# A two-layer hybrid decoder step on one core: the order of the work in both mixes is set anew

## What is computed

```python
def trunk_layer(x, ...):
    h = x @ p['w_in']                                   # 1024 -> 2560, 20 tiles of 128 rows
    u_a, q_b, k_b, v_b, q_c, k_c, v_c, g_c = split(h)   # 2,2,2,2,2,2,4,4 tiles
    ya = rms_norm(s5_branch(u_a, ...))                  # complex diagonal scan, gelu, h*sigmoid(h@w_glu)
    yb = rms_norm(sb_attend(q_b, kb, vb, sb_bias))      # stick-breaking attention, samples read paged K/V
    yc, ret_s = retention_branch(q_c, k_c, v_c, g_c)    # rotary, decay, state, group norm, silu(g)*o
    x = layer_norm(ALPHA * x + concat(ya, yb, yc) @ p['w_out'])
    f = conv_ffn(x, prev, w_up, conv_w, conv_b, w_down) # 1024 -> 5632 -> 2816 -> 1024
    return layer_norm(ALPHA * x + f)
```

## Time and profile before

| | |
|---|---|
| runs, median (lowest to highest) | 739.29 us (739.11 to 741.52), 3 runs |
| the profiled execution | 739.12 us, its span 737.3 us, mean granted clock 0.977 |
| TensorE busy | 678.6 us |
| VectorE busy | 557.2 us |
| ScalarE busy | 407.9 us |
| GpSimd busy | 173.6 us |
| first mix, input norm included | 0 to 142.1 us |
| second mix, from its first raw unit | 377.0 to 498.2 us |

### The profile page before, as it was taken

One profiled execution on the slowest core, in us unless ns is written; L12 is line 12 of the kernel. 1 busy time (PEld: TensorE's weight loads), 2 busy tenths in 40 slices (PEclk: granted clock), 3 DMA queues, 4 the chain that ended last, 5 costly groups with the idle time before them and its releaser, 6 DMA issues. The chain is left out here.

```text
span 737.3 us, 13093 instructions
## 1 busy us (share of the span) xinstructions
PE 678.6 (92%) x4950; PEld 623.7 (85%) x4950; DVE 557.2 (76%) x1083; ACT 407.9 (55%) x649; POOL 173.6 (24%) x130
## 2 busy tenths in 40 slices
PE   5999988597999999998999979969899999999994
PEld 4877776496999999997997768759699999999993
DVE  6688975968988888599945997256899888873543
ACT  4766514747666666652367643374576666664343
POOL 0000000344222222644220000024432221245441
PEclk9999999799999999999999999998999999999998
DMA  9666530342756554533347462241375555546511
GB/s 352 192 222 228 169 106 30 115 148 92 235 200 241 181 190 174 184 144 140 146 160 255 164 213 90 88 171 57 116 245 201 176 193 176 183 168 209 170 58 59
DMA packets 43728, 122.41 MB, mean 166 GB/s; under 512 B 5186, under 2 KB 16354, under 8 KB 43154
## 3 DMA queue, kind: packets, MB, share of 16 engines
q1 hardware_dynamic: 39746, 115.55, 45.1%
q0 software_dynamic: 704, 3.06, 1.4%
q10 hardware_dynamic: 3216, 2.97, 1.2%
HBM read 116.05 MB, written 5.51 MB: 165 GB/s over the span
## 5 line engine op out<-in xcount | busy, mean ns | idle before, releaser
L388 PE MATMUL ps<-x_hi,w_hi 128*128 128x264 f32 x688 | 196.1, 285 | 1.1 <-DVE x_lo L1650 1.1
L389 PE MATMUL ps<-x_lo,w_hi 128*128 128x264 f32 x688 | 194.9, 283 | 0.0
L390 PE MATMUL ps<-x_hi,w_lo 128*128 128x264 f32 x688 | 194.8, 283 | 0.0
L835 ACT CAST w_hi<-ring 128x1024 fp32r<-128x1024 f32 x146 | 151.2, 1041 | 78.4 <-PE ps L390 77.3
L1267 DVE TENSOR_TENSOR w_lo<-ring,w_hi 128x1024 fp32r<-128x1024 f32 x114 | 141.5, 1243 | 39.8 <-ACT w_hi L835 36.8
L381 PE MATMUL ps<-x,ring 128*128 128x264 f32 x576 | 135.6, 391 | 4.5 <-ACT x L923 4.5
L381 PEld LDWEIGHTS ps<-x,ring 128*128 128x128 f32 x576 | 106.2, 190 | 30.4 <-issue 9.1
L388 PEld LDWEIGHTS ps<-x_hi,w_hi 128*128 128x128 f32 x688 | 129.5, 188 | 1.9 <-DVE x_lo L1650 1.5
L389 PEld LDWEIGHTS ps<-x_lo,w_hi 128*128 128x128 f32 x688 | 129.6, 188 | 0.1
L390 PEld LDWEIGHTS ps<-x_hi,w_lo 128*128 128x128 f32 x688 | 129.0, 187 | 0.0
L1719 POOL TENSOR_TENSOR w_lo<-ring,w_hi 128x1024 fp32r<-128x1024 f32 x32 | 78.2, 2450 | 136.9 <-ACT w_hi L835 136.9
(11 more groups left out here) (305 smaller groups left out, 1052.4 us busy)
## 6 DMA issues: line engine op xcount, KB each, us to landing
ring<-in_units SPq DMA_DIRECT2D x188, 512.0 KB, 3.5
kv<-in_kpool SPq DMA_DIRECT2D x32, 128.0 KB, 2.4
kv<-in_vpool SPq DMA_DIRECT2D x32, 128.0 KB, 2.6
SR<-in_sret SPq DMA_DIRECT2D x2, 1024.0 KB, 6.0
out_rsample<-SR POOLq DMA_DIRECT2D x2, 1024.0 KB, 8.0
z<-in_xT SPq DMA_DIRECT2D x2, 528.0 KB, 5.3
out_kv<-hb ACTq DMA_DIRECT2D x2, 528.0 KB, 4.1
out_y<-x SPq DMA_DIRECT2D x2, 528.0 KB, 2.6
```

The costliest lines, as they stand in the source:

```text
L388: mm(out, wh, hi, start=start, stop=False)
L389: mm(out, wh, lo, start=False, stop=False)
L390: return mm(out, wl, hi, start=False, stop=stop)
L835: E.did(nc.scalar.copy(w_hi[:, split_slot(i)], ring[:, ring_slot(n)]), "w_hi")
```

## The change

It moves steps, and makes one in another way. Nothing in what is computed changes, except for how the value rows get to their place.

1. Layer 0, norm: `s5_angle` and `s5_angle2` behind the eight differences; `s5_den` and the third part of the phases in front of `ln_tail_raw`; the fourth part right behind it. ScalarE takes the sines of the constants behind tile 5, and makes the tables of the first half right behind the norm.
2. S5's input projections follow units 5, 6, 9, 10 in layer 0 (before 7, 8, 12, 13) and 2, 3, 6, 7 in layer 1 (before 3, 4, 8, 9), so in layer 1 the first stands within the raw units. `raw_add` of unit 2 comes later.
3. The tables of the second half lie in a place of their own (over RI and KD) and their low part over VT. For layer 1 the turns are made in the down projection of layer 0: ScalarE behind splits 12 to 15, VectorE behind the last residual.
4. All other steps follow other units. The sums rms and gvar now follow unit 18, so unit 19 stands behind them.
5. Silu is taken for three gate tiles ahead of the evacuation of unit 19 and for the fourth behind it (semaphore gsil counts 2); the first four branches are split ahead of the inverse root of the group norm. VectorE's `gn_out` and `branch_lo` alternate. `split_lo` of the fourth w_out unit moves behind them.
6. VS, vs_scratch and the transfers go. `v_samples` multiplies, for each sample and head, a column of v repeated 32 times with the identity; ScalarE copies the two banks to VBC.

```diff
-OUT_BANK = [3, 4, 6, 7]
+OUT_BANK = [4, 5, 6, 7]
-TAB_AT = [(7, 9), (None, 7)]
-TURNS_AT = [(3, 4), (4, 5)]
+TURNS_AT = [[5, 6, 6, 7], [12, 13, 14, 15]]
-AT = [{"ss": 5, "sc": 6, "b00": 7, "b01": 8, "vbt": 9, "b10": 12, "b11": 13, "c0": 13, "vt": 16, "tails": 16,
-       "c1": 18, "glu": 19, "inner": 19, "kt": 19, "values": 19, "rsq": 19, "rt": 19, "out": 19, "sv": 19,
-       "yt": 19, "gmean": 19, "gvar": 19, "rms": 19},
-      {"b00": 3, "b01": 4, "ss": 5, "sc": 6, "b10": 8, "b11": 9, "c0": 9, "vbt": 10, "tails": 12, "c1": 14,
-       "glu": 15, "inner": 16, "kt": 16, "vt": 16, "values": 16, "rsq": 16, "rt": 17, "out": 17, "sv": 17,
-       "yt": 18, "gmean": 18, "gvar": 19, "rms": 19}]
+AT = [{"b00": 5, "b01": 6, "ss": 6, "sc": 7, "tab": 8, "vbt": 8, "b10": 9, "b11": 10, "c0": 10, "logs": 10, "srg": 12,
+       "tails": 14, "c1": 15, "glu": 16, "inner": 17, "kt": 17, "values": 17, "sv": 17, "rsq": 17, "vt": 16,
+       "rt": 18, "yt": 18, "out": 18, "vb": 18, "gmean": 18, "rms": 18, "gvar": 18},
+      {"b00": 2, "b01": 3, "ss": 4, "tab": 4, "sc": 5, "b10": 6, "b11": 7, "c0": 7, "logs": 7, "vbt": 8, "srg": 12,
+       "tails": 10, "c1": 11, "glu": 13, "inner": 13, "kt": 13, "values": 14, "sv": 14, "rsq": 14, "vt": 15,
+       "rt": 15, "yt": 15, "out": 16, "vb": 17, "gmean": 17, "rms": 17, "gvar": 18}]
...
+            def v_samples(L):
+
+                for half in range(2):
+                    bank = claim(2 + half, "vbev", L, half + 1)
+                    for b in range(4):
+                        for h in range(HEADS):
+                            v = hb[:, VC + h, SEQ + 4 * half + b:SEQ + 4 * half + b + 1].to_broadcast([P, 32])
+                            ins = mm(bank[32 * h:32 * h + 32, b * DV:(b + 1) * DV], v, C["ident"], start=True, stop=True,
+                                     tile_position=(0, 32 * h))
+                    E.did(ins, "vb")
...
+                if AT[L]["b00"] < RAW:
+                    s5_evac(L, 0, 0)
+                    neg_c(L)
                 correction(2)
-
-            def s5_turns_up(L, part):
-
-                if part == 0:
+                if L == 0:
+                    s5_tables(L, 0)
+
+            def s5_turns_up(L, jj):
+
+                if jj == 0:
                     act.wait_ge(S("turned"), L + 1)
-                    if L > 0:
-                        need(act, "bb", L, 1)
-                    E.settle()
+                    need(act, "bb", L, 1)
...
             def v_spread(L):
-                act.wait_ge(S("st_vs"), 16 * (L + 1))
-                v4 = vs_dram[L].rearrange("b (h e) -> h b e", h=HEADS)
-                for h in range(HEADS):
-                    act.dma_start(VBC[32 * h:32 * h + 32], v4[h:h + 1].to_broadcast([32, NS, DV])
-                                  ).then_inc(S("ld_vbc"), 16)
+                for half in range(2):
+                    need(act, "vb", L, half + 1)
+                    E.did(nc.scalar.copy(VBC[:, 4 * half:4 * half + 4], ps[:, 2 + half].rearrange("p (b e) -> p b e", b=4)),
+                          "vbev")
...
+                    if i == at_["gvar"]:
+                        for k in range(4):
+                            branch_hi(L, k)
                         need(act, "gvar", L, HEADS)
                         E.did(f(rg[:], ps[:, 4:8, 0:T], ACT.Ln, bias=eps_t[LN_EPS]), "gv1")
                         E.settle()
                         E.did(f(rg[:], rg[:], ACT.Exp, scale=-0.5), "gr")
-                E.settle()
-                E.did(f(hb[:, GC:GC + HEADS], hb[:, GC:GC + HEADS], ACT.Silu), "gsil")
-                for k in range(KT):
+                        E.did(f(hb[:, GC:GC + 3], hb[:, GC:GC + 3], ACT.Silu), "gsil")
+                E.settle()
+                E.did(f(hb[:, GC + 3], hb[:, GC + 3], ACT.Silu), "gsil")
+                for k in range(4, KT):
                     branch_hi(L, k)
+                split_hi(L, N_IN + 3)
...
                         if d in S5_ACT:
                             s5_params(L + 1, S5_ACT.index(d))
+                        for jj in range(HJ):
+                            if d == TURNS_AT[1][jj]:
+                                s5_turns_up(L + 1, jj)
...
-                split_lo(L, N_IN + 2)
-                split_lo(L, N_IN + 3)
                 s5_cat(L)
                 sb_cat(L)
-                gn_out(L)
-                for k in range(4, KT):
-                    branch_lo(L, k)
+                split_lo(L, N_IN + 2)
+                gn_scale(L)
+                gn_out(L, 0)
+                gn_out(L, 1)
+                branch_lo(L, 4)
+                gn_out(L, 2)
+                branch_lo(L, 5)
+                gn_out(L, 3)
+                branch_lo(L, 6)
+                branch_lo(L, 7)
+                split_lo(L, N_IN + 3)
...
+                if L + 1 < DEPTH:
+                    s5_turns_down(L + 1)
             ln_tail(2 * DEPTH)
```

More of the change, by code:

```diff
@@ L196, in hybrid_step @@
         ps = ctx.enter_context(nc.psum_tensor("ps", [P, 8, 512], F32))
-        vs_dram = [nc.dram_tensor(f"vs_scratch{l}", [NS, HEADS * DV], F32, kind="Internal").ap()
-                   for l in range(DEPTH)]
         def pv(L, name, i=0, n=1):
@@ L713, in _ @@
                         vb_transposes(L)
-                    if L == 0 and i == at_["vt"]:
-                        transposes(L)
                     if i == at_["tails"]:
@@ L721, in _ @@
                         s5_glu(L)
+                    if L == 0 and i == at_["vt"]:
+                        transposes(L)
                     if i == at_["inner"]:
@@ L725, in _ @@
                         k_transposes(L)
-                    if L > 0 and i == at_["vt"]:
-                        transposes(L)
                     if i == at_["values"]:
                         sb_values(L)
+                    if i == at_["sv"]:
+                        sb_sample_values(L)
                     if i == at_["rsq"]:
@@ L873, in ln_raw @@
                     square(q, t)
-                if L == 0:
-                    s5_params(0, 2)
-                    logs()
+                    if L == 0 and t == 5:
+                        s5_params(0, 2)
+                        logs()
                 rate(q)
@@ L1028, in _ @@
                     E.did(nc.scalar.copy(hb[:, i], ps[:, in_bank(i), 0:T]), "in_evac")
-                    for part in range(2):
-                        if i == TURNS_AT[L][part]:
-                            s5_turns_up(L, part)
                     if i == 3:
@@ L1047, in _ @@
                                     neg_c(L)
-                    if i == at_["b11"]:
-                        sb_logs(L)
-                    for hf in range(2):
-                        if i == TAB_AT[L][hf]:
-                            s5_tables(L, hf)
+                    if L == 0:
+                        for jj in range(HJ):
+                            if i == TURNS_AT[0][jj]:
+                                s5_turns_up(L, jj)
                     if i == at_["ss"]:
@@ L1082, in _ @@
                         E.did(f(sg[:], ps[:, 2:4, 0:T], ACT.Sigmoid), "sig")
-                    if L > 0 and i == at_["vt"]:
+                    if L == 0 and i == at_["vt"]:
                         v_tokens(L)
-                        v_spread(L)
+                    if i == at_["sv"]:
+                        need(act, "sbys", L, 1)
+                        E.did(nc.scalar.copy(ysb[:], ps[:, 3].rearrange("p (a b) -> p a b", a=2)), "ysev")
                     if i == at_["rsq"]:
@@ L1488, in ret_states @@
                 need(dve, "srg", L, 1)
-                dve.wait_ge(S("ld_vbc"), 64 * (L + 1))
+                need(dve, "vbev", L, 2)
                 for b in samples:
@@ L1555, in gn_out @@
                     E.did(stt(Oh[:, h], Oh[:, h], pv(L, "gn_g", h), rg[:, h], ALU.mult, ALU.mult))
-                need(dve, "gsil", L, 1)
                 E.settle()
-                for h in range(HEADS):
-                    E.did(stt(hb[:, GC + h], Oh[:, h], pv(L, "gn_b", h), hb[:, GC + h], ALU.add, ALU.mult), "catc")
+            def gn_out(L, h):
+                need(dve, "gsil", L, 1 + h // 3)
+                E.did(stt(hb[:, GC + h], Oh[:, h], pv(L, "gn_b", h), hb[:, GC + h], ALU.add, ALU.mult), "catc")
             def branch_lo(L, k):
@@ L1582, in residual @@
                 E.did(stt(z[:, i], x[:, i], ALPHA, bank, ALU.mult, ALU.add), "z")
-            for part in S5_PARTS[:3]:
-                part(0)
+            s5_rates(0)
             needq(dve, "lnc", 0, 1)
@@ L1590, in _ @@
                 ln_diff(0, t)
+            s5_angle(0)
+            s5_angle2(0)
             s5_turns(0)
-            s5_phases(0, 0, 0)
-            s5_phases(0, 0, 1)
+            s5_den(0)
+            for part in range(3):
+                s5_phases(0, 0, part)
             for L in range(DEPTH):
@@ L1596, in _ @@
                 if L == 0:
-                    for part in S5_PARTS[4:]:
-                        part(0)
-                    s5_phases(0, 0, 2)
```

(15 more changed lines are left out.)

90 lines of the change are left out of this document (45 added, 45 removed).

## The result

The changed kernel takes 729.1 us (median; 728.9 to 729.2) where the kernel before took 739.2 in the same session: a ratio of 0.9862, 95% interval 0.9833 to 0.9891. It is 10.1 us faster; 17.9 had been forecast. The range of 712 to 733 holds it, and the sign is right, but almost half of the gain is missing.

What follows compares the result with a forecast made beforehand. TensorE was taken as the bound: 739.1 us minus 34.9 of waits and low clock, plus 7.6 + 4.8 new waits, 1.7 clock, 2.8 value rows, 0.1 norm, gives 721.2 us; range for 8 in 10, 712 to 733.

Steps and rivals of the forecast that it cites:

- The ceiling: Both mixes: 26.8 us of TensorE waits plus 8.1 of low clock, 34.9 us that are not TensorE's work.
- part 1: Layer 0 norm: S5 denominator and third phase step fill VectorE's idle time before the variance; costs 0.1 us.
- Part 2: Layer 0 mix, S5 earlier: masked scores at 86.3 instead of 94.5 us; 7.6 us of new TensorE waits.
- The clock drop of 1.7: Layer 0, behind the two waits at unit 10: low clock costs 1.7 us, bounds 0 and 1.7.
- Part 3: Layer 1 mix, S5 earlier: masked scores at 431.5 instead of 439.6 us; 4.8 us of new waits, no clock drop.
- Part 4: Value rows by TensorE in both layers: 64 rows take 2.0 us, net cost 1.4 per layer, 2.8 in all.
- No cover is left at that place: At the value rows, their net TensorE cost counts in full: 1.4 us per layer, 2.8 in all.
- Part 5: End of each mix: unit 19 and four early branches cover ScalarE's chain; both 7.2 us waits and slow starts go.
- The down projection: Down projection of layer 0: no net change in time, bounds -2 and +2 us.
- the prediction's own sign of being wrong: Down projection: the prediction is wrong if w_lo waits grow beyond their 4.3 us; one of three signs named.
- The slower rival: Down projection: ScalarE parks for bb, splits come late and the clock stays low; 748.0 us, chance 0.09.
- the wait only moves: Output product: ScalarE's closing chain still sets its start, 14.5 + 4.7 us stay; 740.4, no change, chance 0.06.

Runs made afterwards that it cites:

- run 1: Changed kernel, but ScalarE evacuates unit 19 ahead of the first Silu and its table load; 723.95 us.
- run 3: Changed kernel with unit 19 evacuated ahead of the Silus and the turns of layer 1 behind splits 16 to 19; 719.65 us.
- run 6: Changed kernel with the value rows made the former way, by four small transposes and a trip through memory; 727.97 us.
- run 11: Run 5 with the low halves of the down projection's units 14 and 16 made by VectorE instead of GpSimd; 716.48 us.
- run 10: Changed kernel with the low halves of the down projection's units 14 and 16 made by VectorE instead of GpSimd, both layers; 723.01 us.
- run 4: Changed kernel with turns behind splits 16 to 19, but ScalarE still waits for bb behind split 12; 726.45 us.
- run 8: Run 5 with first-half tables (layer 0) and second-half tables (layer 1) behind awaited evacuations, and down-projection phase steps one unit later; 720.91 us.
- run 9: Run 8 with the down projection's phase steps back where run 5 has them, so only the tables moved; 718.71 us.
- run 5: Run 3 with layer 0's second S5 input projection of the second half, first output projection, logarithms, tails, c1, glu and v turns one unit later; 717.94 us.
- run 12: Run 11 with the turns back behind splits 12 to 15, as in the changed kernel; 715.87 us.
- run 2: Changed kernel with ScalarE's turns of layer 1 behind splits 16 to 19 instead of 12 to 15; 723.23 us.

## Why the prediction was right in sign and too high in gain

**The ceiling and part 1** held. The first product starts at 8.98, and the variance is taken up at 23.49 without idle time (forecast 23.4).

**Part 2.** The places were right, the sizes mostly high: 0.85 at unit 5 (forecast 1.2), 0.34 for bb (0.2), 1.79 and 0.75 behind unit 10 (1.7 and 1.0), nothing at the tails (0.8), 0.48 at the gelu product (1.5), 1.25 for RI (1.2): 5.5 us for 7.6. The clock drop of 1.7 came as taken, but that was luck in part: in runs 1 and 3 the same two waits stand at the same place and the clock stays at 1.00 behind them. There TensorE waits 0.77 at the tails and 1.10 at the gelu product, which is nearer to the forecast 0.8 and 1.5. So the low clock had mostly used up waits that would have come anyway: unit 19 ends at 133.7 in the changed kernel and at 133.9 in run 1, and counting both was counting twice. The rows that I set against it were misread too: the four waits before the group norm add up to 4.2 us, not 3.8. Two waits of before that I left out of the ceiling, 0.49 and 0.80 us around the sample retention, went as well, 1.3 more gained.

**Part 3.** 0.41 for the sample scores (1.4), 1.27 (1.5), 2.11 at the tails (1.9): 3.8 for 4.8, and no clock drop, as said. "None is long enough for a clock drop by the rows" doesn't hold, though: behind the same 2.11 it came in runs 3, 6 and 11.

**Part 4.** 64 rows in one block:

```profile
122.61 1.95 PE L513 MATMUL ps<-cst,hb 128*32 128x128 f32 x64
```

That is 0.03 us each, as forecast from the retention rows; at the full-width price it would be 7. Here trace and page differ. The Trainium skill ("TensorE: Matmul & The Clock Gate", Part 3, The mechanism) lets a load overlap a running matmul only where the row group differs; these 64 all use the same rows, and the load rows (1.69 us in all) lie within the product rows. That the four column places work side by side would give the same time, since four such rows take 0.12 us, about what one full-width row does (0.11); these rows don't part the two. "No cover is left at that place" held as far as run 6 can tell: about 2.5 us for both layers by the trace with the chance clock drop taken out, for 2.8.

**Part 5** missed a reader. I followed rsqrt, table, Silu and the fifth cat_lo, and counted "the evacuation and last Silu by X+6.8" as a link of that chain. But the product's first unit, due at X+3.7 behind unit 19, writes the bank that this evacuation reads. With X = 130.0 the trace gives the evacuation's end at 136.6, X+6.6: my number was right and I didn't ask who else waits for it. That is 2.92 + 1.23 us of waits and 1.7 of clock, 5.9 us (run 1 gets 5.2 back by the medians, 3.1 by the ratios). The rival "the wait only moves" had named this in part, that ScalarE's closing chain still sets the product's start; it had put 7.2 us per layer on it where 2.92 and 1.23 were left.

**The down projection** was "put at 0, bounds -2 and +2". It cost 5.4, outside the bounds, and with it the prediction's own sign of being wrong came true: the w_lo waits grew beyond their 4.3 us, to 9.0. The slower rival had the right place and the right engine and a wrong price. It said that "11 us of delay are covered", counting from split 12 to VectorE's w_lo 13, and that beyond this each split comes a turn late. ScalarE was parked 9.54 us, so by its own rule nothing should have happened. What neither the sum nor the rival had is the third engine. GpSimd makes every second low half. Behind a parked ScalarE its splits come in one bunch, beside VectorE's phase steps, and these then take 3.3 us each and hold up the w_lo of unit 15. Run 10 shows it. In run 4 the two phase steps kept their 1.23 us, and a split met the w_lo itself (3.36 us). The trace of before already shows the effect, in two rows that I hadn't put side by side (GpSimd, then VectorE):

```profile
339.61 2.39 POOL L1719 TENSOR_TENSOR w_lo<-ring,w_hi 128x1024 fp32r<-128x1024 f32 x1 [3.73 <-ACT w_hi L835]
...
339.63 2.65 DVE L1338 TENSOR_TENSOR bb<-disc,s5b 128x256 f32<-128x256 f32 x1
```

A VectorE step of this size beside no split takes 0.43. This one is 2.2 us late for it, 8 us ahead of the wait of 2.4 in the earlier trace rows; that the one makes the other is argued, not shown. The Trainium skill has the rule ("SBUF — State Buffer", Who interferes with whom): a VectorE instruction with both inputs in SBUF and a GpSimd instruction that reads SBUF exclude each other for a whole instruction. The trace agrees in the main: the step begins 0.02 us after the split and ends behind it, though only by 0.28 us of its own 0.43. I had not weighed that page, and it bore on this change more than the two that I cited.

**Unsettled.** That GpSimd's sums and VectorE's turn steps hold each other up in run 8 is read from its rows and not tested. No run undid the norm's part alone.

**The balance.** The bank (5.9 us) and the down projection (5.4) took 11.3 us. Smaller waits than forecast (2.1 in layer 0, 1.0 in layer 1) and the two waits left out of the ceiling (1.3) gave 4.4 back, which leaves 6.9 of the 7.3 that are missing. That the time fell within 712 to 733 owes something to this: neither of the two large terms was in the sum, and errors the other way made up for part of them.

## What to carry to other kernels

When a chain is reordered, list for every buffer in it all that wait for it to come free, the next stage's first write above all; a table load ahead of an evacuation is paid by whoever claims that bank. When an engine is made to wait ahead of work that feeds others, ask not only how late each piece comes but which pieces then come together, and on which engines they run side by side: here the lateness was free and the bunching cost 5 us. And a wait has two prices, its length and the low clock that may follow it: two waits of 1.0 and 1.6 us cost 2.6 here, one of 2.35 cost 1.7 more than it says wherever the drop came. Since the drop behind waits of about 2 us comes in one execution and not in the next, compare two traces only after adding up (1 - clock) x length in both.

## What was not expected of the hardware

A VectorE step with two SBUF inputs that began beside a GpSimd split ended a little behind the split, by 1.1 us for a step of 1.23 and by 0.3 for one of 0.43. So steps of 1.23 took 3.2 to 3.4 us, and steps of 0.43 took 2.65 and 1.72. Steps that read PSUM kept their 0.43 us beside the same splits.

The granted clock fell behind waits of 1.95 (0.66 over 4.6 us in run 9), 2.34 (0.63 in run 5), 2.92 (0.69) and 6.76 us (0.59), and behind the pair of 1.79 and 0.75 (0.55 and 0.60). It stayed at 1.00 behind 2.11 in layer 1 and behind 1.6 in runs 10 and 12. But the same wait at the same place goes either way from one execution to the next. Windows of run 1 behind the pair, of run 9 behind a wait of 2.34, and of run 3 behind the 2.11:

```profile
69.30:75.30 6.00, 5.22 (x40) 3.73 (x41) 5.84 (x14) 5.29 (x5) 0.00 (x0) 1.00 0.66 199
...
335.00:339.60 4.60, 4.50 (x37) 4.50 (x38) 4.25 (x10) 1.43 (x3) 2.30 (x1) 1.00 0.66 226
...
420.90:426.90 6.00, 6.00 (x31) 5.54 (x32) 5.97 (x6) 0.00 (x0) 0.00 (x0) 0.72 0.59 186
```

The clock is full behind the pair and behind the 2.34, where it had fallen in other traces, and low behind the 2.11, where it had stayed up. So neither the length of a wait nor its place decides alone; what else does, the runs don't show. Leaving out the last 25 us of each span, the profiled executions lost from nothing (run 12) to some 8 us (runs 2 and 6) in this way, which is not far from what the whole change gained.
